# A two-path decoder step on one core: sample keys' copy and score product moved, norm gains on their own semaphore, decode's key turns over three PSUM banks

## What is computed

```python
def mlstm_layer(x, g, w_in, b_i, b_f, hnorm, w_out, c0, n0, m0):
    p = rmsnorm(x, g) @ w_in
    q, k, v, o, z, gi, gf = jnp.split(p, [...], axis=-1)
    ...
    hc = jax.nn.sigmoid(heads(o)) * hc                     # hc: mlstm_cell(q, k / sqrt(d), v, gates, state)
    hc = head_rmsnorm(hc, hnorm.reshape(H_A, DH_A))
    y = (hc.reshape(bsz, t_, D_A).astype(x.dtype) * jax.nn.silu(z)) @ w_out
    return x + y, c1, n1, m1

# inside mlstm_cell, per chunk:
a = jnp.exp(d - mj[..., None]) * jnp.einsum('bhjd,bhsd->bhjs', qc, kc)
num = w_inter[..., None] * jnp.einsum('bhvk,bhjk->bhjv', c, qc) + jnp.einsum('bhjs,bhsv->bhjv', a, vc)

def diff_mix(q, k_parts, v_parts, masks, lam):
    ...                                                     # scores of both halves c = 0, 1 of each head
    p = jax.nn.softmax(jnp.concatenate(scores, axis=-1), axis=-1)
    w = p[:, :, 0] - lam * p[:, :, 1]
    ...                                                     # out = w @ values
```

## Time and profile before

| | us |
|---|---|
| median of 3 runs | 1901.7 (1901.42 to 1903.68) |
| the profiled execution's own time | 1898.74 |
| its span in the profile | 1896.6 |
| PE busy | 1703.2 (90%) |
| PE weight loads | 1384.7 (73%) |
| DVE busy | 1042.4 (55%) |
| ACT busy | 839.5 (44%) |
| POOL busy | 320.4 (17%) |

### The profile page before, as it was taken

The page is one execution under the profiler, slowest core; times in us unless marked ns, Lnnn a source line. Parts: engine busy times, 40 slices in busy tenths (PEclk is TensorE's granted clock), DMA queues, the critical chain, the costliest instruction groups (busy, mean ns, idle before and its releaser), DMA issues. The chain is left out here.

```text
span 1896.6 us, 31172 instructions
## 1 busy us (share of the span) xinstructions
PE 1703.2 (90%) x9243; PEld 1384.7 (73%) x9243; DVE 1042.4 (55%) x2696; ACT 839.5 (44%) x1994; POOL 320.4 (17%) x814
## 2 busy tenths in 40 slices
PE   4299999999999997997999999999999588887798
PEld 3287887878788785777878778778788466665476
DVE  4534445444443444344777767767766466676443
ACT  5244434333343332243555545555545366665322
POOL 1011212212121120010122221221222012111101
PEclk8699999999999997998999999999999789898799
DMA  5123050340413103132211211211100567767713
GB/s 154 36 56 72 22 92 2 90 81 11 92 14 78 27 11 135 52 129 63 61 56 40 65 50 42 58 54 44 39 23 26 200 228 259 272 227 237 263 58 110
DMA packets 164757, 171.97 MB, mean 91 GB/s; under 512 B 14634, under 2 KB 133834, under 8 KB 164658
## 3 DMA queue, kind: packets, MB, share of 16 engines
q1 hardware_dynamic: 161538, 170.78, 30.6%
q10 hardware_dynamic: 3120, 0.01, 0.1%
HBM read 141.85 MB, written 28.91 MB: 90 GB/s over the span
## 5 line engine op out<-in xcount | busy, mean ns | idle before, releaser
L1016 PE MATMUL PS<-WH,XH 128*128 128x512 f32 x512 | 212.5, 415 | 0.0
L1016 PE MATMUL PS<-WH,XL 128*128 128x512 f32 x512 | 201.9, 394 | 0.0
L1016 PE MATMUL PS<-WL,XH 128*128 128x512 f32 x512 | 201.9, 394 | 0.0
L1997 PE MATMUL PS<-W,XH 128*128 128x512 f32 x384 | 123.8, 403 | 0.0
L2423 PE MATMUL PS<-cst,RAW 128*128 128x128 f32 x512 | 87.3, 322 | 40.5 <-DVE XL L2330 34.9
L1751 ACT ACTIVATE WORK<-PD,WORK 128x896 f32<-128x896 f32 (+7 forms) x128 | 94.9, 741 | 62.7 <-DVE WORK L1918 57.6
L1016 PEld LDWEIGHTS PS<-WH,XL 128*128 128x128 f32 x512 | 96.2, 188 | 22.8
L2423 PEld LDWEIGHTS PS<-cst,RAW 128*128 128x128 f32 x512 | 68.5, 165 | 58.7 <-DVE XL L2330 42.6
L1016 PEld LDWEIGHTS PS<-WH,XH 128*128 128x128 f32 x512 | 96.7, 189 | 19.8
L1016 PEld LDWEIGHTS PS<-WL,XH 128*128 128x128 f32 x512 | 96.8, 189 | 17.1
L2330 DVE TENSOR_TENSOR XL<-PS,XH 128x512 fp32r<-128x512 f32 x128 | 83.9, 684 | 38.2 <-ACT XH L2251 38.1
(11 more groups left out here) (361 smaller groups left out, 4575.4 us busy)
## 6 DMA issues: line engine op xcount, KB each, us to landing
RAW<-in_cache_k SPq DMA_DIRECT2D x64, 512.0 KB, 4.7
WORK<-in_cache_v SPq DMA_DIRECT2D x64, 512.0 KB, 4.6
RAW<-in_w_in_a SPq DMA_DIRECT2D x40, 512.0 KB, 7.0
out<-WORK SPq DMA_DIRECT2D x16, 512.0 KB, 3.0
out<-RAW SPq DMA_DIRECT2D x16, 512.0 KB, 3.2
RAW<-in_w_in_b SPq DMA_DIRECT2D x60, 128.0 KB, 2.3
RAW<-in_w_kv SPq DMA_DIRECT2D x56, 128.0 KB, 2.3
WORK<-d_G SPq DMA_DIRECT2D x8, 528.0 KB, 12.1
```

The lines of the kernel that those rows point to most:

```text
L1016: last = nc.tensor.matmul(bank, x[:, k, tok(t, P)], wkvoz(w)[:, k, :], start=(k == i == 0), stop=(k == KT - 1 and i == 2))
L1997: last = nc.tensor.matmul(out, x[:, k, at(NT - 1 - s)], w[:, k, cols], start=(k == i == 0), stop=(k == KT - 1 and i == 2))
```

## The change

Three things, in three phases.

1. In the norm phase the three loads of norm weights count on a semaphore of their own, `gains`. POOL and PE wait for the constants alone, ACT for `gains` where it first uses gA.
2. In the mLSTM phase the copy of the sample tile's turned keys stands before `squares` on ACT, and the sample tile's `scores` behind the query half (1, A) on PE.
3. In decode the half turns go over three banks, BK[0], BK[1] and BK[7]. The turn of the softmax weights, which used BK[7], is a member of the same round (`TURNS`). A table, `T_LAST`, gives for each the previous user of its bank, and each waits for that one.

```diff
-            sq, rr, xs, tp, hi, lo, pch, g_ld, g_zero, g_hi = (
-                sem(f"na_{s}") for s in ("sq", "rs", "xn", "tp", "hi", "lo", "pool", "gw", "zero", "ghi"))
+            sq, rr, xs, tp, hi, lo, pch, g_ld, g_zero, g_hi, gains = (
+                sem(f"na_{s}") for s in ("sq", "rs", "xn", "tp", "hi", "lo", "pool", "gw", "zero", "ghi", "gains"))
...
-                            act.dma_start(g[:, :], v.rearrange("(k p) -> p k", p=P)).then_inc(consts_in, 16)
+                            act.dma_start(g[:, :], v.rearrange("(k p) -> p k", p=P)).then_inc(gains, 16)
...
-                            act.wait_ge(consts_in, 64)
+                            act.wait_ge(gains, 48)
...
-                    pool.wait_ge(consts_in, 64)
+                    pool.wait_ge(consts_in, 16)
...
-                    pe.wait_ge(consts_in, 64)
+                    pe.wait_ge(consts_in, 16)
...
                         if not first:
+                            keys_turned(g, NT)
                             squares(g, NT - 1)
                             tail(g)
                             exponential(g, NT)
-                            keys_turned(g, NT)
                             states(g, 0)
...
                             project_queries(h, 0, B)
-                        if not first:
-                            scores(g, NT)
                         if not last:
                             project_queries(h, 1, A)
                         if not first:
+                            scores(g, NT)
                             past(g, 0)
...
+            TURNS = [u for u in range(10)] + ["W"] + [u for u in range(10, 16)]
+            T_BANK = {u: BK[(0, 1, 7)[n % 3]] for n, u in enumerate(TURNS)}
+            T_LAST = {u: TURNS[n - 3] if n >= 3 else TURNS[(15, 16, 14)[n]] for n, u in enumerate(TURNS)}
...
                             for j in range(2):
-                                wait(pe, kl, 2 * PAGES * b + (2 * p + j - 1))
+                                u = 2 * p + j
+                                before = T_LAST[u]
+                                if before == "W":
+                                    wait(pe, wr, b)
+                                else:
+                                    wait(pe, kl, 2 * PAGES * (b if before < u else i) + before + 1)
                                 for h in range(4):
-                                    x = nc.tensor.transpose(BK[j][:, h * P:(h + 1) * P],
+                                    x = nc.tensor.transpose(T_BANK[u][:, h * P:(h + 1) * P],
...
                             pe.wait_ge(wd, i + 1)
+                            if keys:
+                                pe.wait_ge(kl, 2 * PAGES * b + T_LAST["W"] + 1)
+                            else:
+                                pe.wait_ge(kl, 2 * PAGES * b)
```

More of the change, by code:

```diff
@@ L2251, in k_high @@
                                 act.activation(XH[:, 4 * j:4 * j + 4, p * P:(p + 1) * P],
-                                               BK[j].rearrange("p (h t) -> p h t", h=4), ACT.Copy).then_inc(kh, 1)
+                                               T_BANK[2 * p + j].rearrange("p (h t) -> p h t", h=4), ACT.Copy).then_inc(kh, 1)
                         def v_high(p):
@@ L2329, in k_low @@
                                 cols = (slice(None), slice(4 * j, 4 * j + 4), slice(p * P, (p + 1) * P))
-                                v.tensor_tensor(XL[cols], BK[j].rearrange("p (h t) -> p h t", h=4),
+                                v.tensor_tensor(XL[cols], T_BANK[2 * p + j].rearrange("p (h t) -> p h t", h=4),
                                                 XH[cols].bitcast(F32), ALU.subtract).then_inc(kl, 1)
@@ L2370, in weights_low @@
                             v.tensor_reduce(WS[:, 0:PAGES * TS].rearrange("p (a q) -> p a q", q=DS),
-                                            BK[7].rearrange("p (a c q) -> p a q c", c=2, q=DS), AX, ALU.add)
+                                            T_BANK["W"].rearrange("p (a c q) -> p a q c", c=2, q=DS), AX, ALU.add)
                             v.tensor_reduce(WS[0:TS, PAGES * TS:NB * TS].rearrange("p (a q) -> p a q", q=DS),
@@ L2443, in weights @@
                             pe.wait_ge(wd, i + 1)
+                            if keys:
+                                pe.wait_ge(kl, 2 * PAGES * b + T_LAST["W"] + 1)
+                            else:
+                                pe.wait_ge(kl, 2 * PAGES * b)
                             apart(pe)
                             for p in range(PAGES):
-                                nc.tensor.transpose(BK[7][:, p * 64:(p + 1) * 64], SR[0:64, p * P:(p + 1) * P],
+                                nc.tensor.transpose(T_BANK["W"][:, p * 64:(p + 1) * 64], SR[0:64, p * P:(p + 1) * P],
                                                     ident[0:64, 0:64])
```

## The result

The changed kernel's median is 1853.3 us (1851.8 to 1853.5), that of before in the same comparison 1902.5; the ratio is 0.974, 95% interval 0.972 to 0.975. Forecast were 1863.7 us and a range of 1856 to 1876. The direction and the waits that the change takes away were as forecast; the size was 10.4 us short. So the change is worth some 44 to 49 us.

What follows compares the result with a forecast made beforehand. PE, busy 90% of the span, was taken as the bound, so its waits and slow clock count. Norm 4.3, mLSTM waits 13.8, mLSTM clock 7.4 and decode 12.5 make 38.0; 1898.7 becomes 1860.7, plus 3.0 is 1863.7 us, range 1856 to 1876.

Steps and rivals of the forecast that it cites:

- The walk through decode's bank table: Decode: with three banks the score product starts near 1586.0 where the rows allow 1588.2; 2.4 us saved at full clock.
- The median of the runs, 1901.7, is 3.0 above it: Whole kernel: 3.0 us added to 1860.7, since the runs' median lies above the profiled 1898.7; gives 1863.7.
- the clock term: mLSTM head boundaries: half clock at four of seven, 16.7 us of busy PE, goes with the wait; 7.4 us gained.
- The mLSTM sum: mLSTM phase: 13.8 us from the removed waits for the key copy plus 7.4 from the clock.
- The decode sum: Decode: seven sequences at 1.5 us each, 10.5, plus 2.0 for the first sequence; 12.5 us, upper bound 19 to 20.
- the stretch stands still in time while the sequences move against it: Decode: why 1.5 us a sequence was taken, between 0.7 with the half-clock stretch in place and 2.4 at full clock.
- (1): mLSTM: the clock still falls at four boundaries, as three of seven equal waits gave no fall; 7.4 back, 1871.1, 12%.
- (5): mLSTM: past product waits as long as the scores did, clock falls as before; 13.5 + 7.4 back, 1884.6 us, 4%.
- (2): Decode: the low-clock stretch lands on the score product in every sequence; 7 x 0.8 comes back, 1869.3 us, 20%.
- (3): Decode: with less waiting the clock doesn't fall; 7 x 1.0 more gained, 1856.7 us, chance 12%.
- (4): Decode: the transfers bound it, moving 280 GB/s in the low stretch; all 12.5 back, 1876.2 us, chance 6%.
- (6): Decode: slower; PE runs ahead, stands still in one piece, low clock lasts over the products; 1911.3 us, chance 2%.

Runs made afterwards that it cites:

- banks alone: The kernel before with only the decode part, three banks for the half turns; 1885.7 us against 1900.5, ratio 0.992.
- the one with the states first: The changed kernel with ACT's tail and copy of the turned states before the squares in the mLSTM phase; 1852.6 us against 1901.4 for before, ratio 0.974.
- E after K2: The changed kernel with decode's later exponential: it and the softmax shares stand behind the third page of keys; 1842.6 us, ratio 0.969 to before (1900.5).

## Why the prediction fell short

**What held.** Norm: 4.3 forecast, 4.2 and 0.6 measured. The place of each wait and of what comes next: the wait for the key copy is gone, and 0.26 us for the states copy stand where 0.3 was forecast. Heads are 2.2 us shorter where no clock helps, 2.0 forecast. The clock at the boundaries was counted as wholly bound to the wait, and all nine profiles of kernels that have one or both of the mLSTM moves have none of it; the five with the old boundary have 17.0 to 27.3 us. The walk through decode's bank table: 7.7 forecast to the score product, 7.48 measured, and for the later exponential 1.5 us sooner forecast, 1.4 measured. One reading was wrong: the short dips of the clock in slices 3 to 15 aren't in the page, where those slices read 9; only the windows of the earlier trace rows show them.

**Where the 10.4 us lie.** Three steps of the sum were too small: decode by 4.8, what was added for the median by 3.0, the mLSTM part by 2.2; the rest adds 0.4. They all err to the same side. Decode's upper bound of 19 to 20 is inside the range's lower end of 1856 only if every other term stands at its middle, so the range had no room for them together. Against the other median of the changed kernel, 1856.3, the forecast is 7.4 short.

**The step "The median of the runs, 1901.7, is 3.0 above it".** I sized the clock term from one profile, with four falls at seven boundaries, and then added 3.0 us to the result for the difference between profile and median, as if it belonged to the rest of the kernel. Five profiles with the old boundary show 17.0, 17.0, 20.4, 23.8 and 27.3 us of half clock in the mLSTM part, and each 3.4 us is worth about 1.5 (a head lasts 77.9 without, 79.4 with). The first profile was one of the two with the least. What the change takes away there is 21.1 us on average, some 9.3 of time instead of 7.4; so nearly 2 of the 3.0 that I added back were time that the change removes. The changed kernel's own first profile and its median agree to 0.1, but its second profile is 3.2 above its median, so that agreement is partly chance. Where the rest of the 3.0 comes from is open.

**The mLSTM sum, 21.2 for 23.4.** Seven boundaries at 2.25, less 0.6 for the one with a shorter wait, make 15.2, and the last head 0.4; I had 13.8 for all. A dense product is 0.32 us long in the rows and the next starts 0.16 after it, so the idle time that the rows give, counted from the end of the last product, is some 0.16 less than what a wait costs. The rest, 7.8, is the clock's, for which I had 7.4.

**The decode sum, 12.5 for 17.3, the largest.** The walk was right, the clock's part in it was not. The lengths of the inner sequences (from one new-value product to the next) grow with the half-clock time in them, with up to 1.2 us of spread within one line of this table:

| kernel | half clock in a sequence, us | lengths, us |
|---|---|---|
| before, two profiles | 6.8 in all twelve | 33.6 to 34.8 |
| changed, first profile | 0 | 30.9, 30.9 |
| | 3.4 | 32.0, 32.2, 32.4 |
| | 6.8 | 33.0 |
| changed, second profile | 0 / 3.4 / 6.8 | 30.9 / 32.0 to 33.2 / 33.2 |
| banks alone | 0 / 3.4 / 6.8 | 31.6 / 33.0, 33.1 / 33.3 to 34.0 |

The failed step is "the stretch stands still in time while the sequences move against it". I took the stretch of 6.8 us to stay and only its place to vary, and gave its loss 12% as a rival of its own. It varies in length: the first profile of the changed kernel has 17 us in its six inner sequences, where every profile with the old waits has 41. The second error is the size of a sequence at full clock: it gains 3.1 us where I had 2.4 as the upper bound. From the first to the fifth turn it lasts 9.46 us at full clock, not 10.0, because the score product starts 0.25 sooner than walked and takes 2.0 us there, 2.4 before. With 6.8 us of half clock a sequence gains 0 to 1, as walked (0.7). The mean gain of the six is 2.1, so 12.3 us where the sum had 9.0; the stretches ahead of and behind them give 5.0 where it had 3.5. In the second profile, and in the one with the states first, the mean gain is 1.6 and 1.3, about where I had put it (1.5). So a part of the miss is this execution's, and no run says how often each length comes.

**Rivals.** (1) and (5) are refuted, at all seven inner boundaries. (2) happened in single sequences, where the stretch lay on the score product (that of 1612.2 to 1619.0 in the changed kernel's profile), (3) in others. The "seven equal waits" of (1) were not all equal: the seventh is 1.7 us. (4) is refuted by the later exponential, which moves more per second still. (6) didn't occur. The Trainium skill says that the full clock doesn't engage for transposes, since they don't count as busy in the same way ("TensorE: Matmul & The Clock Gate", Part 4: PE-mode transpose). The prediction worked out 6.9 for decode from that, for which its own bounds had 4.9 as the least. Measured were 17.3 in the profile and 14.9 for the banks alone, and with E after K2 the stretch of turns has no fall at all; in the norm phase the clock rose behind 3.4 us in which PE did nothing but turns. So for these 32-bit turns the trace doesn't agree with the Trainium skill.

## To carry to other kernels

In this kernel a wait of the matrix engine of some 2 us cost up to twice its length, because the clock may fall behind it. Whether it does differs from one execution to the next, so size such a term from several profiles, and don't add the gap between profile and median to a forecast whose change removes part of that gap. When a wait is removed, look for the next late step in the same rows and move it too: copies that only need an early result should stand ahead of the ones that wait for another engine. A third buffer helps by the head start it allows, not by being there. Where the reader's own order of work holds the buffers, move what isn't urgent (here the exponential and the softmax shares) behind it.

## What the runs showed of the hardware

- The granted clock fell to 0.50 behind waits of 1.7 to 2.3 us at four to six of seven like places, for 3.4 or 6.8 us, in another set in each of five profiles, two of them of the same program. With waits of 0.44 us and less at the same places it never fell (nine profiles).
- With two halves of head start, decode had 6.8 us of half clock in each of the 42 inner sequences of seven profiles. With three it had 0, 3.4 or 6.8 (30 sequences of five profiles). With the waits ahead of the score product down to 1.5 + 0.2 us it had none (12 sequences of two profiles).
- From 1480 to 1690 us the transfers moved 252 and 247 GB/s in the two profiles of before, 264 in the changed kernel and 275 with E after K2, at a share of 0.79.
